# A two-block transformer on one core: the neighbourhood attention's projections in like pieces, its turns as plain transposes

## The reference, cut to what matters

```
s_nb = q_r . k_win + bias            # 8 x 16 neighbours of each latent
s_cx = q_r . k_c                     # all 256 context positions
p = softmax(concat([s_nb, s_cx]))
o = p_nb . v_win + p_cx . v_c
o_lat = o @ w_out
```

## Time and profile before

| | |
|---|---|
| median of 3 runs | 4180.94 us (4176.02 to 4183.22) |
| profiled execution, its own time | 4184.53 us |
| its span | 4182.5 us |
| TensorE busy | 3833.2 us, 92% |
| VectorE, ScalarE, GpSimd busy | 44%, 32%, 11% |
| mean granted TensorE clock | 0.955 |
| DMA, mean over the span | 76 GB/s |
| neighbourhood attention, first scores to last copy out | 1312.9 to 1631.3 us |

### The profile page before, as it was taken

The page is one execution under the profiler, slowest core; times in us unless marked ns, Lnnn a source line. Parts: engine busy times, 40 slices in busy tenths (PEclk is TensorE's granted clock), DMA queues, the critical chain, the costliest instruction groups (busy, mean ns, idle before and its releaser), DMA issues.

```text
span 4182.5 us, 52761 instructions
## 1 busy us (share of the span) xinstructions
PE 3833.2 (92%) x21504; PEld 2995.4 (72%) x21504; DVE 1851.6 (44%) x2839; ACT 1319.7 (32%) x1950; POOL 459.4 (11%) x379
## 2 busy tenths in 40 slices
PE   7889989999997998999888898899998898889999
PEld 3555657888885887788766666688876666767887
DVE  3556544434334344444533455543333445554333
ACT  4334333313123333323324321232233433124222
POOL 1221201000012120000211220000021122000000
PEclk9999999999998999999999999999999999999999
DMA  5223421211211322222121210233222121113322
GB/s 195 83 90 111 127 95 43 70 61 61 68 49 61 106 71 91 81 95 97 57 55 38 79 46 26 67 93 100 91 67 60 33 75 46 31 50 100 101 91 71
DMA packets 327713, 317.04 MB, mean 76 GB/s; under 512 B 8944, under 2 KB 314000, under 8 KB 327344
## 3 DMA queue, kind: packets, MB, share of 16 engines
q1 hardware_dynamic: 327472, 313.68, 24.0%
HBM read 311.55 MB, written 2.10 MB: 75 GB/s over the span
## 4 chain that ended last, share of the span: by engine, by line
PE 80%; DVE 11%; ACT 4%; issue 2%; POOL 1%; DMA 1%; DVEq 0%; SPq 0%; ACTq 0%; POOLq 0%
PE PS L133 79%; DVE scr L147 5%; ACT scr L143 2%; DVE scr L157 1%; DVE scr L165 1%; DVE PS L161 1%; PE PS L136 1%; ACT L143 1%; DVE NBt L157 1%; DVE scr L169 1%; POOL ring_r L147 1%; DVE scr L177 0%; ACT NBt L143 0%; DVE scr L153 0%; POOL NBt L147 0%
## 5 line engine op out<-in xcount | busy, mean ns | idle before, releaser
L133 PE MATMUL PS<-scr 128*128 128x128 f32 (+7 forms) x7124 | 659.0, 284 | 124.8 <-DVE scr L147 65.0
L133 PEld LDWEIGHTS PS<-scr 128*128 128x128 f32 (+3 forms) x7124 | 512.8, 155 | 268.7 <-issue 103.2
L133 PE MATMUL PS<-ffn_h,ffn_w 128*128 128x512 f32 (+1 forms) x3168 | 616.1, 357 | 7.9 <-DVE ffn_h L157 5.7
L133 PEld LDWEIGHTS PS<-ffn_h,ffn_w 128*128 128x128 f32 x3168 | 524.6, 189 | 100.5 <-issue 9.1
L143 ACT ACTIVATE scr<-PS 128x256 f32<-128x256 f32 (+4 forms) x405 | 187.6, 463 | 740.7 <-PE PS L133 682.2
L133 PE MATMUL PS<-h_h,ring_r 128*128 128x512 f32 (+1 forms) x976 | 357.5, 429 | 38.5 <-POOL ring_r L147 24.6
L133 PE MATMUL PS<-mlp_h,mlp_w 128*128 128x512 f32 x1536 | 361.3, 396 | 0.0
L143 ACT ACTIVATE scr<-scr 128x256 f32<-128x256 f32 (+5 forms) x392 | 194.9, 497 | 524.7 <-DVE scr L157 322.4
L133 PE MATMUL PS<-mlp_g,mlp_w 128*128 128x512 f32 x1536 | 359.7, 396 | 0.0
L133 PEld LDWEIGHTS PS<-mlp_h,mlp_w 128*128 128x128 f32 x1536 | 288.4, 188 | 70.4 <-issue 1.0
L133 PEld LDWEIGHTS PS<-mlp_g,mlp_w 128*128 128x128 f32 x1536 | 288.5, 188 | 69.9
(11 more groups left out here) (153 smaller groups left out, 4739.6 us busy)
## 6 DMA issues: line engine op xcount, KB each, us to landing
ring<-in_ffn_w_in SPq DMA_DIRECT2D x44, 1024.0 KB, 5.0
scr<-in_ada_w SPq DMA_DIRECT2D x52, 768.0 KB, 4.8
ring<-in_w_up SPq DMA_DIRECT2D x32, 1024.0 KB, 5.5
ring<-in_w_down SPq DMA_DIRECT2D x32, 1024.0 KB, 5.3
ring<-in_w_in SPq DMA_DIRECT2D x60, 512.0 KB, 3.9
ring<-in_ffn_w_out SPq DMA_DIRECT2D x16, 1024.0 KB, 5.2
scr<-in_na_bias SPq DMA_DIRECT2D x32, 512.0 KB, 5.1
ring<-in_na_w_qkv SPq DMA_DIRECT2D x24, 512.0 KB, 4.1
```

Of the source, the lines that this page charges most:

```text
L133: return self.eng.matmul(o, lhsT=l, rhs=r, start=start, stop=stop) if self.eng else Nothing()
```

## The change

Four things change, all in this stage:

1. `spread` scales the probabilities in place by the reciprocal of their sums (two VectorE scalings of 128x512 for each item), and `dg` is gone. `flip` turns them with eight plain transposes, each half as soon as its scaling is done.
2. `project` on TensorE goes in pieces of two k-steps for 512 columns and four for 256 (queries 4 slots, latent keys 4, context keys 2, latent values 4), and the context's values are one piece in the last slot.
3. The transposes of a head's values move from the end of its projection into the first slot of its own attention (`turned(tl - 1)`), so `project(8)` exists, for the last head. ScalarE copies them out in the second slot, behind its exponentials of the next item and its split of the value weights.
4. ScalarE copies queries, keys and context keys one slot after their product, and both parts of the values in the last slot. GpSimd's second split moves from slot 10 to 11.

```diff
         def spread(it):
             z = it % 2
             dve.wait_ge(*at("n_ex", it))
-            dve.recip(nst[z][:, 4:6], nst[z][:, 4:6]).then_inc(*dve.up("n_dg"))
-            if it >= 2:
-                dve.wait_ge(*at("nt_full", it - 2, 1))
-            dve.tt(dg[z], bc(ident, 1, 2), bc(nst[z][:, 4:6], 2, 128), ALU.mult).then_inc(*dve.up("n_dg", it))
+            dve.recip(nst[z][:, 4:6], nst[z][:, 4:6]).then_inc(*dve.up("n_sc"))
+            for hf in range(2):
+                dve.ts(Pm[z][:, hf, :], Pm[z][:, hf, :], nst[z][:, 4 + hf:5 + hf], None, ALU.mult, None).then_inc(*dve.up("n_sc", it, hf))
...
         def flip(it):
             z = it % 2
-            pe.wait_ge(*at("n_dg", it))
             for hf in range(2):
+                pe.wait_ge(*at("n_sc", it, hf))
                 o = psum("n_pt", it, 1)[:, 512 * hf:512 * hf + 512]
                 for c in range(4):
-                    t = pe.mm(o[:, c * 128:c * 128 + 128], Pm[z][:, hf, c * 128:c * 128 + 128], dg[z][:, hf, :], True, True)
+                    t = pe.tr(o[:, c * 128:c * 128 + 128], Pm[z][:, hf, c * 128:c * 128 + 128], ident)
                 t.then_inc(*pe.up("nt_full", it, hf))
```

TensorE's new `project` and what it calls:

```diff
+        def product(tl, name, full, wh, wl, t0, tn, per):
+            o, before = cur["rg"].take("na_made", *name)
+            emptied(pe, before)
+            for k in range(8):
+                pe.wait_ge(*at("nl", "na", k, int(t0 == 0)))
+                t = three(o[:, 0:tn], wh, wl, slice(t0, t0 + tn), k)
+                if k == 7:
+                    t.then_inc(*pe.up("na_in_full", *full))
+                if k % per == per - 1:
+                    yield
+
+        def turned(tl):
+            pe.wait_ge(*at("na_made", "n_vt", tl, 1))
             for g in range(3):
                 o, before = cur["rg"].take("na_made", "n_vx", tl, g)
                 emptied(pe, before)
-                pe.wait_ge(*at("na_made", "n_vt", tl, 1))
                 for c in range(3):
                     v = V_AT[3 * g + c]
                     t = pe.tr(o[:, c * 128:c * 128 + 128], VT[:, v:v + 128], ident)
                 t.then_inc(*pe.up("na_in_full", "nvx_full", tl, g))
...
+        def project(tl):
+            if tl:
+                turned(tl - 1)
+                yield
+            if tl == 8:
+                return
+            pe.wait_ge(*at("na_lo", "qk", tl))
+            for (what, j, (t0, tn)), per in zip(NQK, (2, 2, 4)):
+                o_ = 0 if what == "q" else 1024
+                yield from product(tl, ("n_in", tl, j), ("n_full", tl, j), w8(o_, 1024), w8(2048 + o_, 1024), t0, tn, per)
+            pe.wait_ge(*at("na_lo", "v", tl))
+            for s, (t0, tn) in enumerate(LC):
+                yield from product(tl, ("n_vt", tl, s), ("nv_full", tl, s), w8(4096, 1024), w8(5120, 1024), t0, tn, (2, 8)[s])
```

ScalarE's:

```diff
         def project(tl):
...
+            if tl < 8:
+                split_act("v", tl)
+            if tl:
+                yield
+                for g in range(3):
+                    act.wait_ge(*at("na_in_full", "nvx_full", tl - 1, g))
+                    if tl >= 3:
+                        act.wait_ge(*at("no_full", 4 * (tl - 3) + 3))
+                    act.f(VX[(tl - 1) % 2][:, 3 * g:3 * g + 3, :], psum("na_made", "n_vx", tl - 1, g)[:, 0:384].rearrange("p (c e) -> p c e", c=3),
+                          ACT.Copy).then_inc(*act.up("na_made", "n_vx", tl - 1, g))
+            if tl == 8:
+                yield
+                return
+            for (what, j, (t0, tn)), n in zip(NQK, (4, 4, 2)):
+                yield from idles(n)
+                act.wait_ge(*at("na_in_full", "n_full", tl, j))
...
             if tl < 7:
                 split_act("qk", tl + 1)
...
+            yield from idles(4)
+            values_in(tl, 0)
+            values_in(tl, 1)
+            yield
```

More of the change, by code:

```diff
@@ L1697, in program @@
     PT = [naa(1024).rearrange("p (h c t) -> p h c t", h=2, c=4) for _ in range(2)]
-    dg = [naa(256).rearrange("p (h t) -> p h t", h=2) for _ in range(2)]
     nst = [naa(6) for _ in range(2)]
@@ L1714, in na_turns @@
             if m == 0:
-                bg = project(tl + 1) if tl < 7 else iter(())
+                bg = project(tl + 1)
             spread(it)
@@ L1742, in project @@
             fetch()
-            for _ in range(6):
-                yield
+            yield from idles(6)
             fetch()
-            for _ in range(10):
-                yield
+            yield from idles(10)
         def scores(it):
@@ L1862, in na_act @@
         norm_act(act, "na", LC, ada_gain(1, 0, f_col)[1], na_parts)
[L1864 to L1871, removed]
@@ L1873, in project, with values_in @@
-        def project(tl):
[L1874 to L1878, removed]
-                yield
[L1880 to L1883, removed]
-                yield
-            what, j, (t0, tn) = NQK[2]
-            yield from qk(tl, what, j, t0, tn)
+        def values_in(tl, s):
+            t0, tn = LC[s]
+            act.wait_ge(*at("na_in_full", "nv_full", tl, s))
+            if tl:
+                act.wait_ge(*at("na_in_full", "nvx_full", tl - 1, 2))
+            act.f(VT[:, t0:t0 + tn], psum("na_made", "n_vt", tl, s)[:, 0:tn], ACT.Copy).then_inc(*act.up("na_made", "n_vt", tl, s))
@@ new lines, in project @@
+        def project(tl):
+            if tl < 8:
+                split_act("v", tl)
+            if tl:
+                yield
+                for g in range(3):
[5 more added lines that the diff above has]
+            if tl == 8:
+                yield
+                return
+            for (what, j, (t0, tn)), n in zip(NQK, (4, 4, 2)):
+                yield from idles(n)
+                act.wait_ge(*at("na_in_full", "n_full", tl, j))
+                if tl >= 2:
+                    act.wait_ge(*at("ns_full", 4 * (tl - 2) + 3))
+                act.f(QT[tl % 2] if what == "q" else KTt[tl % 2][:, t0:t0 + tn], psum("na_made", "n_in", tl, j)[:, 0:tn], ACT.Copy,
+                      scale=64 ** -0.5 if what == "q" else 1.0).then_inc(*act.up("na_made", "n_in", tl, j))
@@ L1965, in project @@
         def project(tl):
+            if tl == 8:
+                return
             split_pool("v", tl)
-            for _ in range(10):
-                yield
+            yield from idles(11)
             if tl < 7:
                 split_pool("qk", tl + 1)
-            for _ in range(6):
-                yield
+            yield from idles(5)
         na_turns(project, idle, idle, idle, idle)
```

## The result

The changed kernel takes 4195.15 us (median of 6 runs, 4189.03 to 4197.92), the kernel before 4176.03 in 6 runs. The ratio is 1.0042, with an interval of 1.0028 to 1.0055: slower by 12 to 23 us, with 14 forecast.

What follows compares the result with a forecast made beforehand. TensorE's own work was taken to bound seven heads and VectorE the last. First head -1.9, six heads 6 x 1.8 and last head +5.5 summed to +14.4 us, about 4195 us predicted, range 4180 to 4207.

Steps and rivals of the forecast that it cites:

- The bound of the heads: Seven heads bound by TensorE's own work, 36.1 us a head without any wait; the last head bound by VectorE.
- The scalings: VectorE: two scalings of 0.50 us an item replace one 0.43 us product; 1.40 each beside GpSimd, hidden by 0.3 us.
- The new wait: TensorE waits 5.0 us a head before the query projection for ScalarE's copy of turned values, queued behind exponentials and split.
- V: The moment at which an item's value products start; TensorE was expected to go on after the new wait at V+8.1.
- The clock: The 5.0 us wait brings TensorE to its low clock, costing 2.2 us a head, bounds 0 and 3.2.
- First head: Fourth item's value products at about 1356.8 against 1358.68 before: a gain of 1.9 us, 4.1 without the clock.
- Six heads: Heads between first and last: 43.3 us each, 1.8 more than before, counted as 6 x 1.8 us.
- Last head: Longer copy wait and VectorE loop +3.0 us, fallen clock +2.5 (bounds 0 and 5): +5.5 us.
- The clock holds: Rival: same waits but no low clock stretch, -3.5 us, 4177 us; chance 0.12.
- The wait is short: Rival: copies right after the transposes, wait about 0.9 us, no clock loss, about 31 us less, 4150; chance 0.05.
- GpSimd's lock shows: Rival: fourth item's 0.3 us cover gone or low clock at full bound, up to +12.6 us, 4207; chance 0.07.
- Cheaper transposes: Rival: eight transposes in 0.43 us on TensorE, 14 us less, 4181, no difference; chance 0.02.

Runs made afterwards that it cites:

- experiment 1: Changed kernel with ScalarE's three copies of the turned values moved in front of the exponentials of the head's second item; 4137.75 us, ratio 0.9906 to the kernel before.
- experiment 4: Kernel before with only the scalings and eight plain transposes in place of the diagonal, slots and copies as before; ratio 1.0047 to the kernel before.
- experiment 6: Experiment 4's kernel with GpSimd's split of the next query and key weights waiting for the fourth item's scalings; ratio 1.0009 to the kernel before.
- experiment 2: Changed kernel with the split of the value weights behind the copies instead of in front, exponentials still in front; ratio 1.0010 to the kernel before.
- experiment 3: Changed kernel with 24 unread products of 128x384 behind the nine transposes, inside TensorE's wait; ratio 1.0001 to the kernel before.

## Why the prediction was right, point by point

**The bound of the heads.** Right. TensorE's work in a head without any wait was put at 36.1 us (41.5 - 2.0 - 3.4); the kernel of experiment 1 does it in 36.08. The flips of eight take 1.03 us with the last one's own duration (0.76 + 0.27), so 0.11 each. The Trainium skill's factor of 4 for FP32 transposes (TensorE: Matmul & The Clock Gate, Terms) is not what this kernel gets over its f32 products of the same shape: the trace shows 2 (0.11 against 0.21 us).

**The scalings.** 0.50 us each as taken, 1.01 for both, and 2.4 for two beside GpSimd (2.8 in experiment 4, as the two rows of before said). At the same place of the code two take 2.84 us with GpSimd at work (experiment 4) and 1.01 without (experiment 6), so it is GpSimd's work beside them that costs. The Trainium skill (SBUF — State Buffer, Who interferes with whom) says that one of the two engines has the shared ports for a whole instruction while the other blocks; the trace agrees as far as VectorE goes, and GpSimd hardly loses: its four subtractions take 5.43 us beside the scalings and 5.30 without. That the fourth item covers it was right, too: in the changed kernel TensorE has no wait for it, with 0.8 us to spare where 0.3 were worked out.

**The new wait.** Right in place, releaser and size: 4.88 us for 5.0, each step of VectorE and ScalarE within 0.1 us; TensorE goes on at V+8.17 for V+8.1. Experiments 1 and 2 show the cause, by taking the queue away and by shortening it.

**The clock.** That the wait would bring it down is right, and the average price, too: 2.2 us a head forecast, 2.2 measured by experiment 3. The row 1350.90 to 1356.10 has the clock at 0.83, the 5.1 us of work behind it at 0.51, and then 1.00, much as the earlier trace rows had it. But the forecast took one price for every head. Against the 41.0 us of experiment 3 single heads lost 1.5 to 2.9 us after the same 4.9 us of wait, so that the average met the forecast to the tenth is partly luck. The working also has a slip: 4.8 x 0.48 is 2.3, not 2.2, which would have added less than 1 us to the sum.

**The sum.** First head: -1.9 forecast, -3.1 measured, counted from the norm's last correction to V of its fourth item (69.2 us before, 66.1 after); its wait was 8.1 us, as the working has it (1313.4 to 1321.6), and from the wait's end to V of the fourth item it took 34.2 us for the 35.2 assumed: the clock was low for less of the work. Six heads: +10.8 forecast, 6 x (43.2 - 41.5) = +10.4 measured. Last head: +5.5 forecast, 27.2 - 22.3 = +4.9 measured, from V of the fourth item before it to V of its own fourth: 8.2 us for the first item as worked out (8.1), then 7.4 and 6.5, where the steps give 6.4 before the clock, and 5.0, where they give 4.5. Counted so the stage is 12.2 us longer in the profiled executions, for 14.4 forecast; each of the three terms came out somewhat lower. The runs say 12 to 23; what lies above 12 is not located. The spread of the work ahead of the stage, 12 us between profiles, is enough to hide it. The changed kernel's profiled execution was also one of its two fastest: those two (4189.0 and 4190.5 us) have a mean clock of 0.953 and 0.952 over the whole program, the other four (4194.1 to 4197.9 us) 0.949 to 0.951. Whether more of its heads have the lower clock there isn't shown, as only one execution has a trace.

**The rivals.** *The clock holds* fell to the granted clock of 0.92 to 0.96; experiment 3 is that rival made real in the six heads, though not in the first and the last, and stands at 1.0001 where 4177 was worked out (0.9991 of the median then known). *The wait is short* is experiment 1: it was put at 31 us under before, and it is 39, as the wait went to nothing and not to 0.9 us. *GpSimd's lock shows* didn't happen here, but did in experiment 4, where the cover is missing. *Cheaper transposes* fell: one follows another in 0.11 us.

**What I had wrong** was in the experiments: for experiment 4 I left the clock out after a wait of 3 us, for 2 and 3 I took the clock's price to be alike in all heads, and for 6 I took TensorE's wait in the fourth item to shrink with the scalings. It grew by 0.2 us, as the flip no longer has to wait and TensorE stands longer before the values. Its item is shorter all the same.

## What to carry to other kernels

When a step is moved in an order written for all engines at once, look at what stands in front of it on each engine and at who takes the buffer that it frees: three copies behind the exponentials cost 7 us a head, in front of them nothing. Price a wait of TensorE twice, once as idle time and once as the clock that it brings down: 4.9 us of wait cost 2.2 us more on average, and 4.2 us of useless products in it paid for themselves. A cheaper instruction on a bound engine pays where other work of that engine surrounds it; at the end of a head, with none there, it turned into a longer wait.

## What the runs showed of the hardware

- A TensorE wait of 3.1 to 3.3 us at a head's end went with a lower clock in most heads (0.92 to 0.96 in experiments 4 and 6, 0.99 in one), while waits of 1.5 us in every 5.7 had left it at 1.00. The price of a wait of the same length differs from head to head: 42.5 to 43.9 us a head in the changed kernel with waits of 4.9 us, 41.2 to 42.7 in experiment 2 with waits of 3.7. What decides it stays open.
- Transposes don't bring the clock down where products stand between them: the six heads of experiment 1 have 41 transposes each, at 1.00.
- Two scalings of 128x512 in f32 from SBUF to SBUF take 1.01 us alone, and 2.44 or 2.84 beside GpSimd's subtractions. Four of those take 5.4 to 5.5 us then, and 5.30 without the scalings (experiment 6).
